# A transformer step: the dense layer's norm factor applied to the gate and up sums, its input split chunk by chunk during the output projection

## The reference, cut to what matters

```python
def rmsnorm(x, g):
    y = x32 * lax.rsqrt(jnp.mean(x32 * x32, axis=-1, keepdims=True) + EPS)
    return (y * g.astype(jnp.float32)).astype(x.dtype)

def swiglu(h, w_gate, w_up, w_down):
    return (jax.nn.silu(h @ w_gate) * (h @ w_up)) @ w_down

# even_layer, its end
x = x + jnp.concatenate([y_ssm, y_att.reshape(B, L, D_ATT)], axis=-1) @ w_out
x = x + swiglu(rmsnorm(x, norm_ffn), w_gate, w_up, w_down)
```

## Time and profile before

| | |
|---|---|
| median of 3 runs | 1598.67 us (1596.68 to 1599.17) |
| time of the profiled execution | 1599.5 us |
| its span in the trace | 1596.1 us |
| mean granted TensorE clock | 0.971 |
| PE busy | 1531.1 us, 96% of the span |
| DVE busy | 1289.0 us, 81% |
| ACT busy | 987.3 us, 62% |
| PE's share of the chain that ended last | 85% |

### The profile page before, as it was taken

One profiled execution on the slowest core, in us unless ns is written; L12 is line 12 of the kernel. 1 busy time (PEld: TensorE's weight loads), 2 busy tenths in 40 slices (PEclk: granted clock), 3 DMA queues, 4 the chain that ended last, 5 costly groups with the idle time before them and its releaser, 6 DMA issues.

```text
span 1596.1 us, 23220 instructions
## 1 busy us (share of the span) xinstructions
PE 1531.1 (96%) x7618; PEld 1234.6 (77%) x7618; DVE 1289.0 (81%) x1699; ACT 987.3 (62%) x1294; POOL 110.9 (7%) x156
## 2 busy tenths in 40 slices
PE   6998999899999689999999999999999999999998
PEld 5665454899999478888888888888888888888886
DVE  8978873555543799889989889989889988988986
ACT  5111342444433277787787777777778778777774
POOL 1277600000000000000000000000000000000000
PEclk9998887999999799999999999999999999999999
DMA  6401253345444459989989999999999998999992
GB/s 229 159 27 54 72 161 119 118 160 182 154 145 147 165 182 364 372 309 361 366 320 356 364 347 325 370 347 324 368 355 319 364 375 300 363 369 334 352 357 90
DMA packets 212890, 420.82 MB, mean 264 GB/s; under 512 B 10233, under 2 KB 56469, under 8 KB 212572
## 3 DMA queue, kind: packets, MB, share of 16 engines
q1 hardware_dynamic: 211542, 414.37, 72.8%
q10 hardware_dynamic: 622, 3.45, 0.6%
q0 software_dynamic: 672, 2.32, 0.4%
HBM read 417.50 MB, written 3.07 MB: 264 GB/s over the span
## 4 chain that ended last, share of the span: by engine, by line
PE 85%; DVE 3%; ACT 1%; issue 1%; SPq 0%; DMA 0%; DVEq 0%
PE bank L1313 20%; PE bank L1308 20%; PE bank L1312 20%; PE bank L1171 3%; PE bank L1168 3%; PE bank L1172 3%; PE bank L1333 2%; PE bank L1271 1%; PE bank L1183 1%; PE bank L877 1%; PE bank L1187 1%; PE bank L1186 1%; PE bank L1348 1%; PE bank L1104 1%; PE bank L1148 1%
## 5 line engine op out<-in xcount | busy, mean ns | idle before, releaser
L2198 DVE TENSOR_TENSOR split<-raw_w,split 128x1024 fp32r<-128x1024 f32 x672 | 787.7, 1219 | 36.6 <-ACT split L1701 32.6
L1701 ACT ACTIVATE split<-raw_w 128x1024 fp32r<-128x1024 f32 x672 | 689.0, 1060 | 121.9 <-PE bank L1308 119.9
L1308 PE MATMUL bank<-split,xgr 128*128 128x512 f32 x896 | 358.1, 400 | 3.8 <-DVE xgr L2262 3.8
L1313 PE MATMUL bank<-split,xgr 128*128 128x512 f32 x896 | 354.2, 395 | 0.0
L1312 PE MATMUL bank<-split,xgr 128*128 128x512 f32 x896 | 354.0, 395 | 0.0
L1308 PEld LDWEIGHTS bank<-split,xgr 128*128 128x128 f32 x896 | 169.2, 189 | 42.0 <-DVE split L2198 4.3
L1313 PEld LDWEIGHTS bank<-split,xgr 128*128 128x128 f32 x896 | 168.9, 188 | 39.7
L1312 PEld LDWEIGHTS bank<-split,xgr 128*128 128x128 f32 x896 | 169.2, 189 | 37.9
L1308 PE MATMUL bank<-split,hbr 128*128 128x512 f32 x448 | 178.0, 397 | 0.0
L1313 PE MATMUL bank<-split,hbr 128*128 128x512 f32 x448 | 177.0, 395 | 0.0
L1312 PE MATMUL bank<-split,hbr 128*128 128x512 f32 x448 | 176.8, 395 | 0.0
(11 more groups left out here) (418 smaller groups left out, 1962.1 us busy)
## 6 DMA issues: line engine op xcount, KB each, us to landing
raw_w<-in_moe_gate SPq DMA_DIRECT2D x112, 1024.0 KB, 5.5
raw_w<-in_moe_up SPq DMA_DIRECT2D x112, 1024.0 KB, 6.1
raw_w<-in_moe_down SPq DMA_DIRECT2D x112, 1024.0 KB, 5.5
ring<-in_w_gate SPq DMA_DIRECT2D x11, 1024.0 KB, 5.2
ring<-in_w_up SPq DMA_DIRECT2D x11, 1024.0 KB, 7.5
ring<-in_w_down SPq DMA_DIRECT2D x8, 1408.0 KB, 6.5
ring<-in_w_in SPq DMA_DIRECT2D x5, 2048.0 KB, 9.2
ring<-in_w_out SPq DMA_DIRECT2D x2, 2048.0 KB, 8.7
```

Source lines behind the costliest of these rows:

```text
L1308: first = mm(out, hi, place[:, s, 0, cols], start=start, stop=False)
L1313: last = mm(out, hi, place[:, s, 1, cols], start=False, stop=stop)
L1701: A(place[:, s, 0, :], raw_w[:, at:at + BLOCK], ACT.Copy).then_inc(sem("high_ready"), 1)
L2198: TT(place[:, s, 1, :], raw_w[:, at:at + BLOCK], place[:, s, 0, :].bitcast(F32), ALU.subtract).then_inc(sem("low_ready"), 1)
```

## The change

The factor of the norm (one number for each token) is taken out of the dense layer's input and put behind its first products: PE multiplies the weights with `x * g`, and DVE multiplies each gate sum and each up sum with the factor `rs` as it reads them from PSUM. So the dense layer's input no longer depends on the sums of squares, and its high and low parts are made chunk by chunk in the loop over the output projection's fills, right behind each chunk's residual (`dense_in`). For chunks 4 to 7 the next block of weights is split after that (`OUT_LEAD`), for chunks 0 to 3 before it. In the dense loop silu now reads SBUF and waits for DVE's product, and DVE does three multiplications for each pair instead of one. The 8 scalings of `norm(1)`, the 8 high copies behind them and the 8 low parts behind those are gone. Buffers move: the high and low parts of the input now take the place that the squares had, the squares take the early place, and the `hist` buffer moves. The counts of `normed` fall by C.

```diff
--- before.py
+++ after.py
@@ -265,6 +265,7 @@
 FF_AHEAD = 3
 FF_BLOCKS = 2 * FT
 OUT_BLOCKS = C
+OUT_LEAD = 4
 
 
 DOWN_CUTS = [(0, 8), (8, 16), (16, FT)]
@@ -457,7 +458,7 @@
         after = SLOT * RING - PLACES * 2 * BLOCK + FF_PLACES * 2 * BLOCK
         sq_early = low[:, FT * T:FT * T + C * T].rearrange("p (c t) -> p c t", c=C)
         sq_ffn = ring[:, after:after + C * T].rearrange("p (c t) -> p c t", c=C)
-        sqs = [sq_early, sq_ffn, sq_ffn, sq_early]
+        sqs = [sq_early, sq_early, sq_ffn, sq_early]
         tk, at = carve(low, 2 * FT * T)
         std, rs = tk(T), tk(T)
         ffa = tk(4 * T).rearrange("p (r t) -> p r t", r=4)
@@ -469,8 +470,8 @@
         tk, at = carve(low, FT * T + C * T + 6 * T)
         pl = tk(C * T).rearrange("p (c t) -> p c t", c=C)
         assert at[0] <= 2 * FT * T, at
-        hist = ring[:, after + 2 * C * T:after + 2 * C * T + C * NB * 15].rearrange("p (c b r) -> p c b r", c=C, b=NB)
-        assert after + 2 * C * T + C * NB * 15 <= SLOT * RING
+        hist = ring[:, after + 12 * T:after + 12 * T + C * NB * 15].rearrange("p (c b r) -> p c b r", c=C, b=NB)
+        assert after + 12 * T + C * NB * 15 <= UT_AT + 4 * T
         ext = low[:, 2 * C * NP_:2 * C * NP_ + C * NB * 16].rearrange("p (c b r) -> p c b r", c=C, b=NB)
         pnew = low[:, FT * T + C * T + 2 * T:FT * T + C * T + 2 * T + D]
         assert 2 * C * NP_ + C * NB * 16 <= FT * T and D <= 4 * T
@@ -484,9 +485,15 @@
         hb5 = hbr[:, :].rearrange("p (r h f s) -> p r h f s", r=2, h=2, f=4)
         place = split[:, :].rearrange("p (s h n) -> p s h n", s=PLACES, h=2)
 
-        xs = split[:, FF_PLACES * 2 * BLOCK:FF_PLACES * 2 * BLOCK + 2 * C * T].rearrange(
-            "p (h c t) -> p h c t", h=2, c=C)
-        assert FF_PLACES * 2 * BLOCK + 2 * C * T <= PLACES * 2 * BLOCK
+        xs_at = FF_PLACES * 2 * BLOCK
+        xs_far = UT_AT + 4 * T - (SLOT * RING - PLACES * 2 * BLOCK)
+        assert xs_at + 12 * T <= UT_AT - (SLOT * RING - PLACES * 2 * BLOCK) and xs_far + 4 * T <= PLACES * 2 * BLOCK
+
+        def dense_in(half, c):
+
+            at = xs_far + (c - 4) * T if half and c >= 4 else xs_at + (half * C + c) * T
+            return split[:, at:at + T]
+
         th = tk(2 * 512).rearrange("p (r k) -> p r k", r=2)
         hb = tk(2 * 512).rearrange("p (r k) -> p r k", r=2)
         xrow = tk(D)
@@ -1165,11 +1172,11 @@
                     for c in range(C):
                         if n == 0:
                             pe.wait_ge(sem("xs_low"), c + 1)
-                        first = mm(out[:, 0:T], w[0][:, c, :], xs[:, 0, c, :], start=(c == 0), stop=False)
+                        first = mm(out[:, 0:T], w[0][:, c, :], dense_in(0, c), start=(c == 0), stop=False)
                         if c == 0:
                             first.then_inc(sem("ff_begun"), 1)
-                        mm(out[:, 0:T], w[0][:, c, :], xs[:, 1, c, :], start=False, stop=False)
-                        last = mm(out[:, 0:T], w[1][:, c, :], xs[:, 0, c, :], start=False, stop=(c == C - 1))
+                        mm(out[:, 0:T], w[0][:, c, :], dense_in(1, c), start=False, stop=False)
+                        last = mm(out[:, 0:T], w[1][:, c, :], dense_in(0, c), start=False, stop=(c == C - 1))
                     last.then_inc(full((kind, f)), 1)
             for co in range(C):
                 out = open_fill(("down", co))
@@ -1632,7 +1639,7 @@
 
             def hidden_high_part(f):
 
-                emptied(act, ("up", f))
+                act.wait_ge(sem("hidden"), f + 1)
                 A(hff[:, 0, f, :], ffa[:, 2 + f % 2, :], ACT.Copy).then_inc(sem("hidden_high"), 1)
 
             def ff_high(n):
@@ -1648,27 +1655,27 @@
                   unit(name, 256)[:, k * C:(k + 1) * C, (f % 2) * P:(f % 2) * P + P], ACT.Copy
                   ).then_inc(sem("ff_high_ready"), 1)
 
-            def out_ready(c):
-
-                n = c + FF_AHEAD
+            def block_high(n):
+
                 if n < OUT_BLOCKS:
                     out_high(n)
                 else:
                     ff_high(n - OUT_BLOCKS)
+
+            for c in range(C):
+                if c < OUT_LEAD:
+                    block_high(c + FF_AHEAD)
                 emptied(act, ("wout", c))
-
-            squares(1, out_ready)
+                A(dense_in(0, c), x3[:, c, :], ACT.Identity, scale=param("g_ffn0")[:, c:c + 1]).then_inc(sem("xs_high"), 1)
+                A(sqs[1][:, c, :], x3[:, c, :], ACT.Square).then_inc(sem("squares"), 1)
+                if c >= OUT_LEAD:
+                    block_high(c + FF_AHEAD)
             root(1)
-            for c in range(C):
-                act.wait_ge(sem("normed"), C + c + 1)
-                A(xs[:, 0, c, :], h3[:, c, :], ACT.Copy).then_inc(sem("xs_high"), 1)
             for f in range(FT):
                 for n in (2 * f + FF_AHEAD, 2 * f + FF_AHEAD + 1):
                     ff_high(n)
-                filled(act, ("gate", f))
-                if f >= 2:
-                    emptied(act, ("up", f - 2))
-                A(ffa[:, f % 2, :], ps(("gate", f))[:, 0:T], ACT.Silu).then_inc(free(("gate", f)), 1)
+                emptied(act, ("gate", f))
+                A(ffa[:, f % 2, :], ffa[:, f % 2, :], ACT.Silu).then_inc(sem("gated"), 1)
                 if f:
                     hidden_high_part(f - 1)
             hidden_high_part(FT - 1)
@@ -2124,26 +2131,46 @@
                 TT(low_, unit(f"ffn{f // 2}", 256)[:, k * C:(k + 1) * C, (f % 2) * P:(f % 2) * P + P],
                    high.bitcast(F32), ALU.subtract).then_inc(sem("ff_low_ready"), 1)
 
-            for c in range(C):
-                n = c + FF_AHEAD
+            def block_low(n):
+
                 if n < OUT_BLOCKS:
                     out_low(n)
                 else:
                     ff_low(n - OUT_BLOCKS)
+
+            def dense_low(c):
+
+                dve.wait_ge(sem("xs_high"), c + 1)
+                STT(dense_in(1, c), x3[:, c, :], param("g_ffn0")[:, c:c + 1], dense_in(0, c).bitcast(F32),
+                    ALU.mult, ALU.subtract).then_inc(sem("xs_low"), 1)
+
+            for c in range(C):
+                if c < OUT_LEAD:
+                    block_low(c + FF_AHEAD)
                 add_residual("wout", c)
-            norm(1, param("g_ffn0"))
-            for c in range(C):
-                dve.wait_ge(sem("xs_high"), c + 1)
-                TT(xs[:, 1, c, :], h3[:, c, :], xs[:, 0, c, :].bitcast(F32), ALU.subtract).then_inc(sem("xs_low"), 1)
+                if c:
+                    dense_low(c - 1)
+                if c == C - 1:
+                    dense_low(c)
+                if c >= OUT_LEAD:
+                    block_low(c + FF_AHEAD)
+            emptied(dve, "norm1")
+            link(nc.vector.reciprocal(rs, std))
             dve.wait_ge(sem("kv_out"), 16 * 2 * TC)
             for f in range(FT):
-                for n in (2 * f + FF_AHEAD, 2 * f + FF_AHEAD + 1):
-                    ff_low(n)
+                ff_low(2 * f + FF_AHEAD)
+                filled(dve, ("gate", f))
+                if f >= 2:
+                    dve.wait_ge(sem("hidden"), f - 1)
+                TT(ffa[:, f % 2, :], ps(("gate", f))[:, 0:T], rs, ALU.mult).then_inc(free(("gate", f)), 1)
+                ff_low(2 * f + FF_AHEAD + 1)
                 filled(dve, ("up", f))
-                emptied(dve, ("gate", f))
                 if f >= 2:
                     dve.wait_ge(sem("hidden_low"), f - 1)
-                TT(ffa[:, 2 + f % 2, :], ffa[:, f % 2, :], ps(("up", f))[:, 0:T], ALU.mult).then_inc(free(("up", f)), 1)
+                TT(ffa[:, 2 + f % 2, :], ps(("up", f))[:, 0:T], rs, ALU.mult).then_inc(free(("up", f)), 1)
+                emptied(dve, ("up", f))
+                dve.wait_ge(sem("gated"), f + 1)
+                TT(ffa[:, 2 + f % 2, :], ffa[:, 2 + f % 2, :], ffa[:, f % 2, :], ALU.mult).then_inc(sem("hidden"), 1)
                 if f:
                     hidden_low_part(f - 1)
             hidden_low_part(FT - 1)
...
```

More of the change, by code:

```diff
@@ L1191, in _ @@
             norm_sums(2)
-            pe.wait_ge(sem("normed"), 3 * C)
+            pe.wait_ge(sem("normed"), 2 * C)
             for i in range(2):
@@ L1226, in _ @@
             for c in range(C):
-                pe.wait_ge(sem("normed"), 3 * C + c + 1)
+                pe.wait_ge(sem("normed"), 2 * C + c + 1)
                 last = mm(out[0:NE, 0:T], rw[:, c, :], h3[:, c, :], start=(c == 0), stop=(c == C - 1))
@@ L2159, in _ @@
             norm(2, param("g_mix1"))
-            dve.wait_ge(sem("normed"), 3 * C)
+            dve.wait_ge(sem("normed"), 2 * C)
             link(nc.vector.tensor_copy(ext[:, :, :, 15:16], h3[:, :, NP_:T].unsqueeze(3)))
@@ L2202, in _ @@
                 low_part(0, n)
-            dve.wait_ge(sem("normed"), 4 * C)
+            dve.wait_ge(sem("normed"), 3 * C)
             link(nc.vector.memset(lgt, 0.0))
```

## The result

The changed kernel takes 1589.34 us in the median of 7 runs (1580.6 to 1590.71), the kernel before 1598.67 us in the median of 7 (1591.09 to 1599.54). The ratio is 0.9941, 95% interval 0.9922 to 0.9959: 9.4 us faster, between 6.6 and 12.5. The prediction was 1590.2 us.

What follows compares the result with a forecast made beforehand. PE, busy all the time in the dense and expert layers, was taken as the bound. Gains of 6.47 + 1.99 = 8.5 us bring the median from 1598.67 to 1590.2 us; range 1586.8 to 1595.6.

Steps and rivals of the forecast that it cites:

- The gap: Between the sums of squares and gate 0: PE's idle time goes, gate 0 follows the sums at once; gain 6.47 us.
- The clock: First 18 dense matmul records behind the gap: they run at full clock, 2.30 us in place of 4.29; gain 1.99 us.
- The rival that the clock falls anyway: At gate 0: the clock falls or comes back late, so only the gap is won, 1592.2 us; chance 0.07.
- The output projection's loop: Output fills: added high and low parts on ACT and DVE stay hidden, blocks having 2.1 us of cover; cost 0.
- the 2.3 us of cover: Before gate 0: the last chunk's low part is done at about 297.2, the sums end at 299.54.
- The factor's new way: Root and reciprocal leave the path; reciprocal over at 302.00, before DVE reads gate 0 about 3.1 us after 299.54; nothing stops.
- The dense loop: Dense layer: two more DVE multiplications for each pair, load 4.2 of 6.14 us, hidden by blocks asked for early; cost 0.
- Transfers and the expert layer: Weight loads: third dense load has 11 us of cover, later ones move with PE's fills, expert layer's too; cost 0.
- Further gaps: Norm 2, pooling and router keep their gaps, 8.5 us earlier; effect 0, with 3.4 us each way for slow-clock stretches.
- The sum: Whole kernel: 6.47 + 1.99 = 8.5 us gained, median 1590.2 us, ratio 0.9947.

Runs made afterwards that it cites:

- e1: The changed kernel, but gate 0 on PE again waits for the reciprocal of the root; 1595.25 us.
- e2: The kernel before, with 13 unused matmuls on PE between the sums of squares and gate 0; 1594.95 us.
- e5: The changed kernel with OUT_LEAD = 0: for all 8 chunks the input's parts and square go ahead of the next block of weights; 1591.69 us.
- e8: The changed kernel with OUT_LEAD = 8: for all 8 chunks the next block of weights is split ahead of the input's parts; 1591.08 us.
- e9: The changed kernel with 3 unused fp32 matmuls of 128x280 in front of the sums of norm 2; 1590.56 us.
- e3_split_at_end: The changed kernel with the input's high and low parts made after the output fills' loop, blocks of weights split in the old order; 1587.54 us.

## Why the prediction was right

**The gap.** Forecast 6.47 us, measured 10.40 - 3.57 = 6.83. The difference is that the idle time counted from the modelled end of the last sum, while the next matmul starts before that. e1 gives the wait back and loses the gain.

**The clock.** Forecast 1.99 us, measured 2.09 over all the dense layer (206.08 us from gate 0 to the sums of norm 2 before, 203.99 after), and 1.9 by itself in e2. The rival that the clock falls anyway is out.

**The output projection's loop.** Forecast at nothing, and it costs nothing: the sums of squares start 25.0 us after the first fill in both. But the steps were sized too small. The high part with a scale for each partition took 0.53 us (forecast 0.44), the low part 0.50 (0.37 to 0.45), and the last residual started 297.92 - 296.69 = 1.23 us after the last fill and not 0.20, because of the loop of 3.46 us. The last low part was done 2.8 us after the sums began and not 1.6; of the 2.3 us of cover 0.8 were left. The forecast of no cost came true with a third of the margin that it had named, and e5 and e8 show that a cost does appear, 0.8 to 0.9 us at gate 0, when the order isn't changed midway.

**The factor's new way.** Forecast: the reciprocal is over 6.4 us after the sums begin (302.00 against 295.60), before DVE reads gate 0 at about 7.0 (302.6). Measured: over at 7.24 (303.93), because the root's table load of 1.28 us (L1430) now stands behind the last block's high part and no longer before the sums end, and the gate product starts at 8.4 (305.11), after one more block's low part. That it costs PE nothing holds as forecast.

**The dense loop.** Forecast 0; gate 0 to down is 135.7 us, without a wait of PE, also with two further additions. DVE's busy time was forecast at 4.2 us for a pair and is 32.86 / 50 x 6.14 = 4.04. A pair's later operations after the change, the answer to the earlier trace rows:

```profile
316.06 0.45 DVE L2165 TENSOR_TENSOR low<-bank,low 128x280 f32<-128x280 f32 x1 [0.63 <-PE bank L1179]
317.34 1.23 DVE L2131 TENSOR_TENSOR split<-ring,split 128x1024 fp32r<-128x1024 f32 x1 [0.83 <-ACT split L1654]
319.14 0.45 DVE L2170 TENSOR_TENSOR low<-bank,low 128x280 f32<-128x280 f32 x1 [0.57 <-PE bank L1179]
319.62 0.45 DVE L2173 TENSOR_TENSOR low<-low 128x280 f32<-128x280 f32 x1
...
317.22 0.42 ACT L1678 ACTIVATE low<-low 128x280 f32<-128x280 f32 x1
```

The gate product (L2165) starts after 0.63 us of waiting for PE, silu (L1678) has its input in time, and the product with it (L2173) follows the up product (L2170) after 0.03 us.

**Transfers and the expert layer.** Forecast 0; PE has no wait for a transfer, and the expert layer takes 1024.1 us where it took 1023.5. The other traces without fillers have 1023.5 to 1024.5, among them kernels built on the changed one at both ends, so this 0.6 us can't be put down to the change.

**Further gaps.** Forecast 0, with 3.4 us in each direction; measured 1.4 us of gain in the traces, which e9 and the comparison of e2 with e5 show to be a matter of the moment in which the clock falls. The Trainium skill (TensorE: Matmul & The Clock Gate, What's actually happening) says that the clock's supervision runs free of the kernel; the traces agree, as the clock falls at different moments of the same gap.

**The sum.** The 8.5 us stood for what the change does, and that measures 6.8 + 2.1 = 8.9 us. That the median's 9.3 lies so near is in part luck: the profiled pair also has 1.1 us lost ahead of the sums, 1.4 won before the router and 0.6 lost behind it, none of which the prediction sized and which nearly cancel.

## What to carry to other kernels

A factor that is the same for all that is summed can go behind the product, and then the reduction that makes it leaves the critical path; look in the trace for what still hides the splitting or casting of the input before making that earlier too. When work of two engines is put into a loop, compare the length of the whole cycle through both with the pace of the third, not only the cover of each item. And count an idle stretch of PE with the slow matmuls behind it: here 6.8 us of waiting cost 8.9, and unused matmuls in three other gaps brought 3.2 us.

## What the hardware showed beside

Executions of one and the same kernel reach the output projection at about 264 or at 269 to 272 us. The stretch from 100 to 140 us, untouched by all edits, in the changed kernel and in e3_split_at_end:

```profile
100.00:140.00 40.00, 40.00 (x185) 25.19 (x184) 31.62 (x62) 7.81 (x29) 31.10 (x40) 0.92 0.15 53
```

```profile
100.00:140.00 40.00, 39.10 (x205) 23.56 (x204) 34.30 (x68) 8.16 (x31) 32.21 (x42) 1.00 0.15 53
```

In 40 us PE gets through 205 matmuls at a granted clock of 1.00 and through 185 at 0.92. The lead of the one over the other goes on growing up to the output projection, where it is 8.0 us (263.68 against 271.69), and it is 8.0 us at the end of the span (1579.4 against 1587.5). The single runs that lie 8 us below the others fit this: 1580.6 us of the changed kernel has a mean clock of 0.978, as e3's profiled run has, where its others have 0.971 to 0.973. That the clock makes all of the 8 us, or what sends an execution into one form or the other, no run here shows. A stage table from one point of the program on is a finer measure here than the total time.

In e1 PE was idle for 3.37 us, and the clock fell not in the idle stretch (granted clock 1.00 from 299.20 to 302.60) but about 0.4 us behind its end. In front of the router of the changed kernel it was the same: 3.16 us idle, the first matmul at 539.76, the granted clock 1.00 from 539.40 to 539.80 and 0.50 from 540.00 to 543.00. So a clock of 1.00 in the idle time doesn't mean that what follows runs at it.
